# Norm factors of queries a and b moved into the exponential, their sums taken by token, rotations on VectorE, latents' squares added by GpSimd

## The chip, the cores and the metric

The kernel runs on one core of a Trainium2 chip. The metric is device time in microseconds (us) of one execution; lower is better. The engines are TensorE (PE, matrix products; PEld is its load of the stationary operand), VectorE (DVE), ScalarE (ACT), GpSimd (POOL) and SyncE (SP, which issues the transfers of the weights).

## The reference, cut to what matters

A first block (pooling, convolutions, gates, a gated feed-forward part) makes x from 256 tokens. Then two layers of a second model run over these 256 latent tokens and 256 context tokens. The change is in the second model's projections and attention:

```python
u = h @ w_in
qa, ka, va, qb, kb, vb, cq, ckv, kpe, z = jnp.split(u, split_points(), axis=-1)
qa = rms(heads(qa, 8), qn_a);  ka = rms(heads(ka, 8), kn_a)      # per head of 64
qb = rms(heads(qb, 12), qn_b); kb = rms(heads(kb, 4), kn_b)
qc = rms(heads(rms(cq, qa_norm) @ w_qb, 6), qn_c)                # cq has 768 columns
kvc = heads(rms(ckv, kva_norm) @ w_kvb, 6)                       # ckv has 512 columns
...
qb = apply_rope2d(qb, cos, sin); kb = apply_rope2d(kb, cos, sin) # latents only
# attention of each head group
s = q @ k * scale (+ bias or mask); p = softmax(s); o = p @ v
```

`rms(x, w)` is `x * rsqrt(mean(x*x) + eps) * w` over a head's 64 columns. Group a adds a position bias to the scores of latents, group b a band mask and a sink per head. Layer 1 needs no context queries, so the queries are 512 tokens wide in layer 0 and 256 in layer 1; keys are always 512 wide.

## The kernel before, in words

Activations lie transposed in SBUF: 128 columns of a head group on the partitions, tokens along the free axis. The weights stream through eight slots of 128x1024 elements (a quarter of a weight block each; SyncE loads a slot as soon as TensorE has used it). To keep precision at the fast rate each quarter is split: ScalarE writes the rounded high part (`whi`, L866), VectorE subtracts for the low part (`wlo`, L1332), and TensorE makes three products a chunk (high by high L2168, high by low of the activations L2169, low by high L2172). An output tile is 128 columns wide and takes two quarters, 48 products; this is a step. ScalarE and VectorE prepare quarters three ahead (`AHEAD`), PSUM has four banks for tiles. Every engine runs one order, written out by Python.

`projections(name, l)` (L600 on) sets that order for stage a (12 tiles: 4 of queries, 4 of keys, 4 of values), b (10 tiles: 6, 2, 2) and c (11 tiles of the latents ckv, kpe and cq, 12 of keys and values, 9 of queries), by lists of items for each step. In c of layer 0, and of layer 1, VectorE also makes products of streamed rows for the conditioning (L1845, L1859).

For every tile of queries and keys in a and b there is a job: VectorE copies the tile from PSUM (L1897), ScalarE squares it (L880) and rounds the square (L882), VectorE (layer 0 and the first group, L1866) or GpSimd (layer 1, L2837) makes the square's low part, TensorE multiplies both by a matrix of ones in two 64-row blocks (L2291, L2292), so that each row of a head holds the head's sum; VectorE takes mean (L1360), ScalarE the root (L895), VectorE the reciprocal (L1363) and the scaling with the gain (L1372). In b a rotation follows: VectorE swaps rows (L1920), GpSimd multiplies by sin and cos and adds (L2845 to L2848). TensorE waits for the eighth rotation before it attends.

The latents' norms (`lora`, jobs ckv and cq) take one full-precision product with ones for each of their 4 and 6 chunks (L2299, two records each), from squares that ScalarE writes into four buffers.

Stage c already takes its sums of keys and queries by token: the squares are the stationary operand, a column or two of ones streams (L2487), so the sums land with tokens on the partitions; a query's factor goes into the exponential as its scale (`q_factor`) and, negated, into the row maximum (`q_minus`).

The attention of a and b lies beside the gates' projections (`z_beside`): for a pair of heads and 128 queries come scores (TensorE, L2521), bias (L1951) or mask (L1958), maximum (L1960, L1966, L1968), exponential (ScalarE, L1224, with its row sum), normalisation (VectorE, L1985), transposes (TensorE, L2532, copied by ScalarE, L1233) and the product with the values (L2547). TensorE waits for a pair's exponential before the next pair's scores.

## Time and profile before

| | us |
|---|---|
| median of 3 runs (3268.28 to 3268.73) | 3268.7 |
| the profiled execution | 3265.98 |
| its span in the trace | 3264.2 |
| TensorE busy | 3220.0 (99%) |
| VectorE busy | 2299.4 (70%) |
| ScalarE busy | 1429.2 (44%) |
| GpSimd busy | 669.2 (21%) |

The table is read so: the span is from the first to the last instruction of one execution. An engine is busy while an instruction of it is under way; matrix products overlap in their pipeline, so a product's own duration is longer than the distance to the next one, and a busy TensorE is not TensorE at its peak. The second model runs from about 1620 us to the end.

### The profile page before, as it was taken

The numbers are of one execution on the slowest core, as the hardware profiler recorded it, in microseconds if no ns is written. First come the engines' busy times: TensorE is split into PE (matmuls) and PEld (weight loads), VectorE is DVE, ScalarE is ACT, GpSimd is POOL, SyncE is SP. The second block draws the span as 40 slices with busy tenths as digits, with TensorE's granted clock in tenths as the row PEclk, the third lists the DMA queues.
The fourth block names the chain that finished last, engine by engine and source line by source line (L and its number), as shares of the span: only waits on it lengthen the run. The fifth ranks groups of instructions, "written<-read, shape, count | busy, mean of one in ns | idle before, by whom it ended". The sixth has DMA issues, their size and how long they took to land.

```text
span 3264.2 us, 56041 instructions
## 1 busy us (share of the span) xinstructions
PE 3220.0 (99%) x20212; PEld 2763.4 (85%) x20212; DVE 2299.4 (70%) x3399; ACT 1429.2 (44%) x2193; POOL 669.2 (21%) x600
## 2 busy tenths in 40 slices
PE   8999999999999999999999999999999999999999
PEld 8999999998998777889888777777878888888878
DVE  7887877567786776777766766566658776776765
ACT  5444445445444343444543433532352363543453
POOL 4999930111450000000300011000001100210000
PEclk9999999999999999999999999999999999999999
DMA  6555555565577777777733222134316553324435
GB/s 220 182 181 185 184 184 187 184 211 187 194 246 258 250 254 256 248 253 244 256 105 113 102 92 83 53 135 140 105 65 213 199 175 113 133 97 142 154 102 177
DMA packets 159873, 559.71 MB, mean 171 GB/s; under 512 B 17552, under 2 KB 23840, under 8 KB 159264
## 3 DMA queue, kind: packets, MB, share of 16 engines
q1 hardware_dynamic: 154144, 534.60, 48.1%
q0 software_dynamic: 5504, 22.04, 2.0%
q8 instruction: 150, 2.46, 0.3%
q14 instruction: 75, 0.61, 0.1%
HBM read 550.26 MB, written 6.31 MB: 171 GB/s over the span
## 4 chain that ended last, share of the span: by engine, by line
PE 89%; DVE 5%; ACT 2%; issue 1%; DVEq 1%; ACTq 0%; DMA 0%; POOL 0%; POOLq 0%; SPq 0%
PE psum L2168 17%; PE psum L2172 17%; PE psum L2169 17%; PE psum L2195 15%; PE psum L2196 7%; PE psum L2379 3%; PE psum L2521 2%; PE psum L2547 2%; PE psum L2532 2%; PE psum L2224 2%; PE psum L2380 2%; DVE wlo L1332 1%; PE psum L2299 1%; DVE rst L1363 1%; DVEq L1318 1%
## 5 line engine op out<-in xcount | busy, mean ns | idle before, releaser
L1332 DVE TENSOR_TENSOR wlo<-raw,whi 128x1024 fp32r<-128x1024 f32 (+3 forms) x844 | 1037.0, 1235 | 379.7 <-ACT whi L866 348.9
L866 ACT ACTIVATE whi<-raw 128x1024 fp32r<-128x1024 f32 (+3 forms) x844 | 863.3, 1029 | 949.9 <-PE psum L2172 465.3
L2168 PE MATMUL psum<-hcat,whi 128*128 128x256 f32 (+1 forms) x3436 | 1122.7, 327 | 4.9 <-DVE wlo L1332 4.2
L2172 PE MATMUL psum<-hcat,wlo 128*128 128x256 f32 (+1 forms) x3436 | 1109.4, 323 | 0.0
L2169 PE MATMUL psum<-hcat,whi 128*128 128x256 f32 (+1 forms) x3436 | 1109.3, 323 | 0.0
L2195 PE MATMUL psum<-hcat,whi 128*128 128x512 f32 x2048 | 724.2, 397 | 0.1
L2168 PEld LDWEIGHTS psum<-hcat,whi 128*128 128x128 f32 x3436 | 653.2, 190 | 72.9 <-issue 16.1
L2172 PEld LDWEIGHTS psum<-hcat,wlo 128*128 128x128 f32 x3436 | 653.1, 190 | 51.4
L2169 PEld LDWEIGHTS psum<-hcat,whi 128*128 128x128 f32 x3436 | 653.5, 190 | 49.4 <-issue 0.7
L2196 PE MATMUL psum<-hcat,wlo 128*128 128x256 f32 x2048 | 573.3, 280 | 0.0
L2195 PEld LDWEIGHTS psum<-hcat,whi 128*128 128x128 f32 x2048 | 384.3, 188 | 105.9 <-issue 17.2
L2196 PEld LDWEIGHTS psum<-hcat,wlo 128*128 128x128 f32 x2048 | 386.6, 189 | 0.1
L2722 POOL TENSOR_SCALAR tap<-glu,par 128x255 f32<-128x255 f32 (+9 forms) x150 | 203.9, 1359 | 0.3 <-issue 0.3
L2379 PE MATMUL psum<-thirdcat,whi 128*128 128x512 f32 x512 | 182.9, 401 | 0.0
L2709 POOL TENSOR_TENSOR thirdcat<-tmp,thirdcat 128x256 fp32r<-128x256 f32 x43 | 51.3, 1194 | 613.5 <-ACT thirdcat L920 613.5
L2724 POOL TENSOR_TENSOR conv<-conv,tap 128x255 f32<-128x255 f32 (+9 forms) x150 | 149.1, 994 | 22.1 <-issue 0.3
L2380 PE MATMUL psum<-thirdcat,wlo 128*128 128x256 f32 x512 | 143.0, 279 | 0.0
L2761 POOL TENSOR_TENSOR racc<-racc,rsq 128x256 f32<-128x256 f32 (+1 forms) x64 | 82.9, 1295 | 240.2 <-ACT rsq L932 215.8
L2379 PEld LDWEIGHTS psum<-thirdcat,whi 128*128 128x128 f32 x512 | 96.1, 188 | 38.9 <-DVE X L1714 9.2
L1363 DVE RECIPROCAL rst<-rst 128x512 f32<-128x512 f32 (+1 forms) x39 | 106.8, 2738 | 25.9 <-ACT rst L895 25.9
L1897 DVE COPY qkv<-psum 128x512 f32<-128x512 f32 (+1 forms) x78 | 49.4, 633 | 81.0 <-PE psum L2172 80.9
L1224 ACT ACTIVATE probs<-psum,stat 128x512 f32<-128x512 f32 (+1 forms) x120 | 72.4, 606 | 70.7 <-DVE stat L1966 70.7
(307 smaller groups left out, 3647.3 us busy)
## 6 DMA issues: line engine op xcount, KB each, us to landing
raw<-in_stream SPq DMA_DIRECT2D x978, 512.0 KB, 3.9
raw<-in_stream SPq DMA_DIRECT2D x18, 384.0 KB, 3.0
raw<-in_stream SPq DMA_DIRECT2D x24, 256.0 KB, 2.9
resid_dram<-X POOLq DMA_DIRECT2D x2, 2048.0 KB, 9.4
crow<-c_dram POOLq DMA_DIRECT2D x4, 1024.0 KB, 9.1
bias<-in_natten POOLq DMA_DIRECT2D x16, 256.0 KB, 2.9
X<-resid_dram POOLq DMA_DIRECT2D x4, 1024.0 KB, 6.2
raw<-in_stream SPq DMA_DIRECT2D x16, 192.0 KB, 2.4
```

The source lines that it names most:

```text
L866: act.activation(whi[:, c % HI_SLOTS, 0:n], raw[:, slot, 0:n], ACT.Copy).then_inc(hi_ready, 1)
L1332: vec.tensor_tensor(wlo[:, slot, 0:n], raw[:, slot, 0:n], whi[:, c % HI_SLOTS, 0:n].bitcast(F32), ALU.subtract).then_inc(lo_ready, 1)
L1363: vec.reciprocal(r, r)
L2168: pe.matmul(dst, h, cat[:, kk, c0:c0 + width], start=(q == 0 and k == 0), stop=False)
L2169: pe.matmul(dst, h, cat[:, kk, c0 + loff:c0 + loff + width], start=False, stop=False)
L2172: last = pe.matmul(dst, l_, cat[:, kk, c0:c0 + width], start=False, stop=(q == nq - 1 and k == nch - 1))
L2195: pe.matmul(psum[:, bank, :].rearrange("p (l c) -> p l c", l=2), h, both, start=first, stop=False)
L2196: return pe.matmul(psum[:, bank, 0:S], l_, both[:, 0, :], start=False, stop=last)
L2379: pe.matmul(psum[:, bank, :], h, thirdcat[:, kk, :], start=first, stop=False)
L2380: return pe.matmul(psum[:, bank, 0:S], l_, thirdcat[:, kk, 0:S], start=False, stop=last)
L2722: pool.tensor_scalar(tap[:, t % 2, 0:S - t], pick(glu, c, 0, S - t), wt, None, ALU.mult)
L2724: pool.tensor_tensor(pick(conv, c, t, S), pick(conv, c, t, S), tap[:, t % 2, 0:S - t], ALU.add)
```

## The change

The queries of a and b are no longer scaled. ScalarE squares a query tile in full precision (in b straight from PSUM, where VectorE's copy then applies the gain), TensorE sums the squares by token (`qcol`), and once per stage VectorE and ScalarE make all factors (`q_factors`, `qstat`). They go into exponential and maximum as in c; the bias of a is multiplied by the factor's inverse instead, one head at a time; the sink needs its own operation. In a the queries' gain goes into the keys' weight. The rotations of b are made by VectorE alone. Of the latents' squares the first is the accumulator, GpSimd adds 3 (ckv) and 4 (cq) others, and TensorE makes 1 and 2 products in place of 4 and 6. Key jobs stay as they were, in both layers two steps behind their tile.

```diff
-        SPLIT = ("qn_a", "kn_a", "qn_b", "kn_b")
+        SPLIT = ("kn_a", "kn_b")
+        LORA_SUMS = {"ckv": (3,), "cq": (2, 3)}
+        LORA_ADDS = {"ckv": (0, 3), "cq": (3, 4)}
...
-                srcs = [whole(qkv[:, base + k, 0:w]) for k in range(count)]
+                srcs = [whole(sq[:, n, 0:w]) for n in LORA_SUMS[name]]
...
+                for t in range(nq_):
+                    at_(t + 1, "qsq", t)
+                    at_(t + 2, "qcol", t)
+                    if name == "b":
+                        at_(t + 1, "rope", ROPES_OF[f"b{l}"][t])
+                at_(nq_ + 2, "qstat")
...
-                at_(4, "sq", ckv, 0, 4, 3)
-                at_(5, "sum", ckv, 0, 4)
+                for m in range(4):
+                    at_(m + 1, "part", ckv, m, l, m)
+                at_(5, "sum", ckv, 0, 1)
...
-                at_(9, "sq", cq, 0, 3, 7)
-                at_(10, "sum", cq, 0, 3)
-                at_(k0, "sq", cq, 3, 6, 10)
-                at_(k0 + 1, "sum", cq, 3, 6)
+                for m in range(6):
+                    at_(6 + m, "part", cq, m, l, 5 + m)
+                at_(k0, "sum", cq, 0, 1)
+                at_(k0 + 1, "sum", cq, 1, 2)
...
+            def q_square(l, name, t, src):
+                n = q_no(name, l, t)
+                if n >= 4:
+                    act.wait_ge(qsq_used, n - 3)
+                act.activation(sq[:, n % 4, 0:chunks_w(l)], src, ACT.Square).then_inc(qsq_ready, 1)
...
+                    elif name == "b" and u < Q_TILES["b"]:
+                        vec.wait_ge(qsq_ready, q_no("b", l, u) + 1)
+                        vec.tensor_scalar(dst[:, j, 0:w], ps, pv("qn_b", l), None, ALU.mult).then_inc(psum_free, 1)
...
+            def q_factors(name, l):
+                k, nq_ = 2 * l + (name == "b"), Q_TILES[name]
+                st = q_mean(nq_, l)
+                nb = chunks_w(l) // P
+                vec.wait_ge(qsq_used, q_no(name, l, nq_))
+                sums_ = psum[:, 6, 0:8 * nq_].rearrange("p (h b) -> p h b", b=4)[:, :, 0:nb]
+                vec.tensor_scalar(st, sums_, 1.0 / HD, EPS, ALU.mult, ALU.add).then_inc(q_mean_ready, 1)
+                vec.wait_ge(q_root_ready, k + 1)
+                if name == "a":
+                    vec.tensor_scalar(q_inverse[:, :, :], st[:, :, 0:2], HD ** 0.5, None, ALU.mult)
+                    fence()
+                vec.reciprocal(st, st)
+                fence()
+                for dst, f in ((q_factor, HD ** -0.5), (q_minus, -HD ** -0.5)):
+                    vec.tensor_scalar(dst[:, 0:2 * nq_, 0:nb], st, f, None, ALU.mult)
+                fence()
...
-                        if r in ROPES_OF[f"b{l}"]:
-                            if it[2] >= 2:
-                                vec.wait_ge(rope_done, it[2] - 1)
-                            vec.stream_shuffle(t, ropes[r], SWAPPED)
-                            vec.drain().then_inc(swapped_ready, 1)
-                            continue
...
-                    vec.scalar_tensor_tensor(ps[:, :, 0:S], bias[:, n % BIASES, :, :], 1.0 / u["scale"], ps[:, :, 0:S],
-                                             ALU.mult, ALU.add)
+                    for h in range(2):
+                        vec.scalar_tensor_tensor(ps[:, h, 0:S], bias[:, n % BIASES, h, :],
+                                                 q_inverse[:, 2 * u["c"] + h, u["q0"] // P:u["q0"] // P + 1],
+                                                 ps[:, h, 0:S], ALU.mult, ALU.add)
...
-                    vec.scalar_tensor_tensor(negmax, top_, -u["scale"], sinks[:, u["sink"]:u["sink"] + 4:3], ALU.mult,
-                                             ALU.min).then_inc(max_ready, 1)
+                    vec.tensor_tensor(negmax, top_, minus, ALU.mult)
+                    fence()
+                    vec.tensor_tensor(negmax, negmax, sinks[:, u["sink"]:u["sink"] + 4:3], ALU.min).then_inc(max_ready, 1)
...
+                        for b in range(chunks_w(l) // P):
+                            last = pe.matmul(psum[:, 6, 8 * t + b:8 * t + b + 8:4], sq[:, n % 4, P * b:P * b + P],
+                                             halves[:, 0::HD], start=True, stop=True)
+                        last.then_inc(qsq_used, 1)
...
-                        if kind == "b":
-                            pe.wait_ge(rope_done, 8 * l + 8)
...
+            def lora_adds(l, name, j):
+                a0, adds = LORA_ADDS[name]
+                acc, w = jobs[j]["srcs"][0][0], jobs[j]["width"]
+                for m in range(1, adds + 1):
+                    a = 7 * l + a0 + m - 1
+                    pool.wait_ge(part_ready, 9 * l + (0 if name == "ckv" else 4) + m + 1)
+                    pool.tensor_tensor(acc, acc, sq[:, a % 2, 0:w], ALU.add)
+                    pool.drain().then_inc(part_used, 1)
+                pool.drain().then_inc(sq_ready, 1)
...
                 if l == 0:
                     pool.wait_ge(gate0_mods, ROW_CHUNKS)
                     crow0_load(1)
+                for name in ("ckv", "cq"):
+                    lora_adds(l, name, JOBS_OF[f"{name}{l}"][0])
```

## Rows read from the trace of the kernel before

**Rows 1.** The page, part 1: busy us (share of the span) and instructions.

```profile
PE 3220.0 (99%) x20212; PEld 2763.4 (85%) x20212; DVE 2299.4 (70%) x3399; ACT 1429.2 (44%) x2193; POOL 669.2 (21%) x600
```

**Rows 2.** Stretches: length, busy us per engine (PE to POOL), clock, DMA share, GB/s.

```profile
2969.00:3075.00 106.00, 105.86 (x608) 92.28 (x604) 69.90 (x94) 33.85 (x46) 0.00 (x0) 1.00 0.51 179
```

**Rows 3.** Timeline, VectorE, a0: start, duration, engine, line, shape [idle before <-releaser].

```profile
1710.98 0.69 DVE L1897 COPY qkv<-psum 128x512 f32<-128x512 f32 x1 [1.80 <-PE psum L2172]
...
1722.37 0.69 DVE L1897 COPY qkv<-psum 128x512 f32<-128x512 f32 x1 [1.80 <-PE psum L2172]
```

**Rows 4.** Timeline, TensorE: the sums of squares in b0 and b1, steps 2 to 9 and 2 to 6.

```profile
1909.46 0.39 PE L2291 MATMUL psum<-sq_hi,halves_r 128*128 128x512 f32 x1
...
1991.78 0.47 PE L2291 MATMUL psum<-sq_hi,halves_r 128*128 128x512 f32 x1 [0.28 <-DVE sq_hi L1866]
...
2817.43 0.28 PE L2291 MATMUL psum<-sq_hi,halves_r 128*128 128x256 f32 x1
...
2823.41 0.28 PE L2291 MATMUL psum<-sq_hi,halves_r 128*128 128x256 f32 x1
...
2844.05 0.36 PE L2291 MATMUL psum<-sq_hi,halves_r 128*128 128x256 f32 x1 [1.07 <-POOL sq_hi L2837]
```

**Rows 5.** Timeline, TensorE, c0: two groups of column sums, 12 products between them.

```profile
2299.98 0.95 PE L2487 MATMUL psum<-con,csq 128*128 128x1 f32 x8
...
2303.66 0.95 PE L2487 MATMUL psum<-con,csq 128*128 128x1 f32 x8
```

**Rows 6.** Timeline, TensorE: the latents' sums, ckv in c0, the first of cq in c1.

```profile
2205.91 3.59 PE L2299 MATMUL psum<-sq,con 128*128 128x512 f32 x8
...
3055.88 1.46 PE L2299 MATMUL psum<-sq,con 128*128 128x256 f32 x6
```

**Rows 7.** Timeline, VectorE, c0: the mean of cq's squares.

```profile
2282.73 0.69 DVE L1360 TENSOR_SCALAR cq_rst<-psum 128x512 f32<-128x512 f32 x1 [0.67 <-PE psum L2299]
```

**Rows 8.** Timeline: GpSimd in a1; VectorE in c1, copy of tile 9 and product.

```profile
2651.07 0.74 POOL L2837 TENSOR_TENSOR sq_hi<-sq,sq_hi 128x256 fp32r<-128x256 f32 x1 [39.42 <-ACT sq_hi L882]
...
3059.12 0.42 DVE L1897 COPY qkv<-psum 128x256 f32<-128x256 f32 x1
...
3059.67 1.30 DVE L1859 CUSTOM_DVE_ANT_0 psum<-raw,crow,gate_half 128x1024 f32<-128x1024 f32 x1
```

**Rows 9.** Timeline, b0: VectorE beside GpSimd; and from the page, part 5, all wlo.

```profile
1976.79 1.81 DVE L1332 TENSOR_TENSOR wlo<-raw,whi 128x1024 fp32r<-128x1024 f32 x1
1977.48 1.72 POOL L2846 TENSOR_TENSOR qkv<-qkv,con 128x256 f32<-128x256 f32 x1
...
L1332 DVE TENSOR_TENSOR wlo<-raw,whi 128x1024 fp32r<-128x1024 f32 (+3 forms) x844 | 1037.0, 1235 | 379.7 <-ACT whi L866 348.9
```

**Rows 10.** Timeline, VectorE: a rotation (c0) from shuffle to end; a small operation (c1).

```profile
2287.63 0.44 DVE L1923 STREAM_SHUFFLE tmp<-cqk 128x256 f32<-128x256 f32 x1
...
2289.48 0.76 DVE L1932 COPY cqk<-cqk 128x512 f32<-128x512 f32 x2
...
3135.45 0.16 DVE L1680 TENSOR_SCALAR q_minus<-col_stat 128x4 f32<-128x4 f32 x1
```

**Rows 11.** Groups by line and shape: count | busy us, mean ns | idle before.

```profile
L1224 ACT ACTIVATE probs<-psum,stat 128x512 f32<-128x512 f32 x80 | 54.0, 677 | 50.2 <-DVE stat L1966 50.2
L1224 ACT ACTIVATE probs<-psum,stat,q_factor 128x512 f32<-128x512 f32 x24 | 18.4, 775 | 5.0 <-DVE stat L1964 4.9
```

**Rows 12.** Timeline: b0, probabilities and transposes; b1, second scores, later exponential and scores.

```profile
2029.11 0.88 DVE L1985 TENSOR_SCALAR probs<-probs,stat 128x512 f32<-128x512 f32 x2
2030.25 1.09 PE L2532 MATMUL psum<-con,probs 128*128 128x128 f32 x8
...
2899.49 1.13 PE L2521 MATMUL psum<-qkv 64*128 64x512 f32 x4 [0.87 <-ACT probs L1224]
...
2921.54 0.19 ACT L1224 ACTIVATION_READ_ACCUMULATOR probs<-psum,stat 128x1 f32 x1
2922.72 1.13 PE L2521 MATMUL psum<-qkv 64*128 64x512 f32 x4
```

More of the change, by code:

```diff
@@ L294, in build @@
     region("consts", CO["invcount"] * 4)
-    region("small", (96 * 2 + KD * 3 + 24 + LAYERS * H_B + S + 120) * 4)
+    region("small", (96 * 2 + KD * 3 + 24 + LAYERS * H_B + S + 192) * 4)
     region("work", 16 * KIB)
@@ L605, in build, with q_no @@
                 vts += [(src[:, base + k, :], k * P) for k in range(count)]
+        Q_TILES = {"a": 4, "b": 6}
+        def q_no(name, l, t):
+            return 10 * l + (4 if name == "b" else 0) + t
         def projections(name, l):
@@ L679, in projections @@
                         at_(q0_ + i + 2, "qfin", i // 3)
-            order = ("sum", "kpe", "fin", "rope", "vt", "cat", "col", "kfin", "spread", "qfin", "sq", "csq", "sqlo")
+            order = ("qcol", "sum", "kpe", "qstat", "fin", "rope", "vt", "cat", "col", "kfin", "spread", "qfin", "qsq", "sq", "part", "csq", "sqlo")
             for u in items:
@@ L890, in squares, with lora_square @@
                     act.activation(sq[p0:p1, n % 4, 0:J["width"]], ap, ACT.Square).then_inc(sq_ready, 1)
+            def lora_square(j, m, l):
+                J = jobs[j]
+                a0, adds = LORA_ADDS[J["name"]]
+                src = qkv[:, LORA_BASE[J["name"]] + m, 0:J["width"]]
+                if m == 0:
+                    act.activation(J["srcs"][0][0], src, ACT.Square).then_inc(part_ready, 1)
+                elif m <= adds:
+                    a = 7 * l + a0 + m - 1
+                    if a >= 2:
+                        act.wait_ge(part_used, a - 1)
+                    act.activation(sq[:, a % 2, 0:J["width"]], src, ACT.Square).then_inc(part_ready, 1)
+                else:
+                    act.wait_ge(part_used, 7 * l + a0 + adds)
+                    act.wait_ge(sq_used, J["src0"] + 1)
+                    act.activation(J["srcs"][1][0], src, ACT.Square).then_inc(sq_ready, 1)
             def root(j):
@@ L1168, in projected @@
                 for u, (s, nq) in enumerate(t[0:2] for t in tiles_):
+                    if name == "b" and 0 < u <= Q_TILES["b"]:
+                        t = u - 1
+                        act.wait_ge(weights_used, tiles_[t][0] + tiles_[t][1] - 1 + SLOTS + 1)
+                        q_square(l, name, t, psum[:, BANK[first + t], 0:chunks_w(l)])
                     hi(SQ.index(s) + AHEAD)
@@ L1172, in projected @@
                             pair(JOBS_OF["hc1"][0], m)
+                    if name == "a" and 0 < u <= Q_TILES["a"]:
+                        act.wait_ge(psum_free, copied(first, u - 1))
+                        q_square(l, name, u - 1, qkv[:, u - 1, 0:chunks_w(l)])
                     for_heads(items[u], first, l)
@@ L1176, in projected @@
                 return items[len(tiles_):]
+            def q_square(l, name, t, src):
[3 more added lines that the diff above has]
+                act.activation(sq[:, n % 4, 0:chunks_w(l)], src, ACT.Square).then_inc(qsq_ready, 1)
             def for_heads(todo, first, l):
-                for it in sorted(todo, key=lambda it: it[0] not in ("sq", "csq")):
+                for it in sorted(todo, key=lambda it: it[0] not in ("sq", "part", "csq")):
                     if it[0] == "fin":
@@ L1205, in for_heads @@
                     elif it[0] == "sq":
+                        name = "b" if jobs[it[1]]["roped"] else "a"
                         act.wait_ge(psum_free, copied(first, it[4]))
+                        act.wait_ge(qsq_used, q_no(name, l, Q_TILES[name]))
                         squares(it[1], it[2], it[3])
+                    elif it[0] == "qstat":
+                        k = 2 * l + (first == T0[f"b{l}"])
+                        nq_ = Q_TILES["ab"[k % 2]]
+                        act.wait_ge(q_mean_ready, k + 1)
+                        st = q_mean(nq_, l)
+                        act.activation(st, st, ACT.Sqrt).then_inc(q_root_ready, 1)
+                    elif it[0] == "part":
+                        act.wait_ge(psum_free, copied(first, it[4]))
+                        lora_square(it[1], it[2], l)
             def probabilities(no):
@@ L2863, in _ @@
                 biases_in(f"a{l}")
-                for n, j in enumerate(JOBS_OF[f"b{l}"]):
-                    if l:
-                        square_low(j)
-                    if n:
-                        rope(l, n - 1)
-                rope(l, 7)
+                for j in JOBS_OF["b1"] if l else ():
+                    square_low(j)
                 if l == 0:
```

81 lines of the change are left out of this document (40 added, 41 removed).

## The prediction

> **What bounds the kernel now.** I read the page first. The engine table [rows 1] shows TensorE with work in flight for 3220.0 of 3264.2 us and VectorE for 70%: what TensorE has to issue, plus the short moments in which it waits, is the time. The table of stretches [rows 2] says the same of one changed stage (context stage of layer 1: 105.86 of 106.00 us at full granted clock). So I read the change as TensorE's work added and removed, and then look at each handover to it: does the new order of VectorE, ScalarE and GpSimd arrive later or earlier than TensorE asks? I call the stages a0, b0, c0, a1, b1, c1 (head group and layer), and a step the time of one output tile.
>
> **Sums of the queries' squares (a and b, 10 tiles per layer).** Before, each tile has two multiplications by the block matrix, as wide as the tile's own. In a0 a step of 48 + 2 such multiplications takes 11.39 us, from one copy to the next [rows 3], so 0.228 each and 0.46 for the two; at half width (layer 1) a step is 5.98 us [rows 4], 0.12 each, 0.24 for the two. After, each tile has 4 (layer 0) or 2 (layer 1) multiplications with the squares as the loaded operand and two columns streaming. The form exists in stage c: from one group of four (eight records) to the next it is 3.68 us with 12 wide multiplications between [rows 5], 12 x 0.228 = 2.73, so a group costs 0.93 to 0.95; half as many cost 0.47. Added: 10 x (0.93 - 0.46) + 10 x (0.47 - 0.24) = 4.7 + 2.3 = **+6.9 us** of TensorE. One column streams there and two here; the weight load is the same, so I keep the value. Bounds: 5 (if the last load hides) and 9 (if each group pays the restart again).
>
> **Latents' squares.** A full-precision sum over one 512-wide chunk: four took 3.59 [rows 6]; less the tail of the last one (about 0.16) that is 0.86 each. At 256 three took 1.46 [rows 6], 0.43 each. Ten sums become three per layer: 7 x 0.86 = 6.0 in c0, 3 x 0.86 + 4 x 0.43 = 4.3 in c1, together -10.3 us. Not all of it reaches the end.
> c0: 2 x 2.57 go at steps 5 and 10, 0.86 comes at step 11, so 4.3 is gained by the end of tile 11. The last sum is 1.7 shorter, but VectorE waited for it only 0.67 [rows 7]; after that its reciprocal and the key rotation set the order as before. VectorE has idle in c0 that covers the earlier start. **-4.95 us** (bounds -6.0 and -3).
> c1: here VectorE is behind. It copies tile 9 at 3059.12 [rows 8], 3.2 us after TensorE has finished it (the sums of step 10 start at 3055.88 [rows 6]). Until now nothing waited for this copy at once; now the first sum of step 11 needs the square of tile 9 and GpSimd's add of it. That add takes at least 0.74 at this width (GpSimd subtracting tiles of the same shape, [rows 8]). In b0 a wlo subtraction that meets a GpSimd product takes 1.81 us, where all 844 have a mean of 1.24, and the GpSimd product 1.72 against 0.74 for a subtraction of its size [rows 8, 9]: they hold each other up. So I let each of the three adds before that copy cost VectorE its 0.74: copy at 3061.3, or 3060.3 if 1 us of its wait for weights goes, since TensorE frees the slots earlier. To the copy come 0.42 for itself, 1.4 for the vector product (1.30 and its fence [rows 8]) that the add has to pass, 0.74 for the add: 3062.9 to 3063.9. Then the sum (0.43) and tile 11 (2.73) end at 3066.1 to 3067.1. Before, tile 11 ended at 3055.88 + 1.30 (three sums) + 5.74 + 2.73 (tiles 10 and 11) = 3065.65. Loss 0.4 to 1.4; without any hold-up it would be a gain of about 2. I take **+0.5 us**, because rows 9 show the hold-up; bounds -3.4 (all of TensorE's saving) and +4.
> The Trainium skill, "SBUF — State Buffer", section "Who interferes with whom", has a rule that speaks against the move: a VectorE instruction with two SBUF inputs and a GpSimd instruction that reads SBUF exclude each other for a whole instruction, whichever began first. By that rule no overlap is left and c1 comes out at its upper end, 1.4; by free overlap it would be -2. The trace agrees with the rule [rows 9].
>
> **VectorE's steps in a and b.** Removed per query tile: mean, wide root round trip, reciprocal, scaling, low half. What that frees matters only where VectorE was late. In b0 TensorE needed 82.32 us for seven steps [rows 4], against 7 x 11.39 = 79.73: 2.6 late. In b1 26.62 us for four steps [rows 4] against 23.92: 2.7 late, and those are query steps. In a0 it was not late: the copy waited 1.80 for TensorE [rows 3].
> After, query steps are light, a rotation on VectorE included (1.85 us from its shuffle to the copy behind it [rows 10]). The first key step isn't: behind the new wait for ScalarE's root of the factors stand the key's mean, root, wide reciprocal, scaling, its rotation, the second wlo and the next key's low half, for which TensorE waits in layer 0. The factors are six operations on 128x48 or less, one 0.16 [rows 10], with one trip to ScalarE: I estimate 1.6 us, between 0.8 (five times 0.16) and 2.7 (0.8 more than a rotation). a0: 11.39 - 1.80 + 1.6 = 11.2: it just fits, **+0.1**. b0: 11.2 + 1.85 + fences = 13.4 against 11.39: TensorE waits 2.0 once, **-2.6 + 2.0 = -0.6** (bounds -2.0 and +1.5). The next step needs no low half; the attention beside the gates starts half a tile later, and VectorE is ready by then. b1: GpSimd makes the low half, nothing waits, **-2.7** (bounds -2.9 and -1).
>
> **What else moves.** ScalarE squares b's queries from PSUM ahead of its whi copy, and VectorE's copy waits for that: some 0.6 us later for whi, wlo and the copy, with two steps of weights and four banks in hand, nothing for TensorE; if that cover were gone, 0.6 a step. GpSimd waits for seven squares a layer; behind it in c0 stands only the load of the context's c row, which the output stage needs, so it is hidden; without that cover it would be the few us of one add. No other transfer moves: the biases and the first rows keep their places.
>
> **Attention of a and b.** An exponential with its scale from a column took 775 ns, with a constant 677 [rows 11]: +0.1 per head, 0.2 per pair. Pairs of b get one more small operation and a fence between maximum and exponential, 0.25; pairs of a with a bias get it in two halves, 0.1. So the chain scores to exponential grows by 0.45 in b and 0.2 to 0.3 in a. Cover: in b1's steady state the scores start 0.99 after the exponential before them has ended [rows 12]: hidden. But the second pair of b1 already waited 0.87 [rows 12], and its successor has little spare: +0.7 in b1, +0.45 in a1 and +0.35 in a0 likewise. In b0 the transposes start 0.26 after the probabilities are scaled [rows 12]; eight pairs are like that, 8 x (0.45 - 0.26) = 1.5. Together **+3.0 us**, bounds +1 and +6.
>
> **Sum.** 6.9 - 4.95 + 0.5 + 0.1 - 0.6 - 2.7 + 3.0 = +2.25 us. The rows are of one execution of 3265.98 us (span 3264.2), 2.7 below the median of the runs shown, 3268.7. The difference is added to the median: **3271.0 us**. What a measurement of this kernel can tell from no change is about 0.2%, 6.5 us: this is within it.
>
> **Rivals.**
> 1. TensorE's own work alone counts and every wait hides. 6.9 - 10.3 - 2.6 - 2.7 = -8.7: 3260.0. For it: 99% busy. Against: VectorE is late in c1 and in b0's first key step, shown above. Chance 0.08.
> 2. GpSimd's lock bites twice. Each add before the copy of tile 9 holds up a second vector instruction (3 x 0.74 = 2.2), and of the three adds of c1 that are twice as wide (an estimate of 1.5 each from [rows 8]) half is not absorbed before step 5, 2.2 more: 3271.0 + 4.4 = 3275.4. Place: copy of tile 9 in c1. It decides once that copy is over 2 us later than now. For it: rows 9, both sides lengthened. Against: in the early steps VectorE waits for weights and can absorb it. Chance 0.14, slower than before, about half of it by over 0.2%.
> 3. The attention chain becomes the bound (the other side, clearly slower). If it grows by more than the 0.99 us of spare in b1, and all of the 0.26 in b0, all 36 pairs of b show their 0.45: 16.2 instead of the 2.2 counted, 3285. It decides when the chain grows by about 1 us per pair, twice my value. For it: rows 12. Against: the parts have rows and add to 0.45. Chance 0.07.
> 4. That the change does not do what it says (the column sums are no cheaper than what they replace) is in my sum already.
>
> **Chances and range.** The forecast's case has 0.71, its own range 3266 to 3275. Faster by over 0.2%: rival 1, 0.07. Slower by over 0.2%: rival 3, 0.07, half of rival 2, 0.07, and 0.03 from the forecast's upper end: 0.17. The rest, 0.76, is within 0.2%. The range of 8 in 10 leaves out rival 3 and most of rival 1 and takes in rival 2: 3264 to 3277.
>
> **What the profile after should show.** Groups of 8 and 4 records of the column sums with 0.93 and 0.47 us to the next tile; b1's query steps at 5.98 + 0.23 without waits; one wait of about 2 us for the low half in b0, at the second key; in c1 a wait of TensorE for GpSimd before the first sum of step 11; wlo at its mean of 1.24 throughout b0 but longer beside the adds; exponentials at 775 ns in all pairs. Wrong would be: no wait at the GpSimd sum in c1 (rival 1), or waits for the exponentials in every pair of b (rival 3).

## The result

| | before | after |
|---|---|---|
| median (lowest to highest) | 3268.24 (3264.88 to 3268.73, 6 runs) | 3284.51 (3281.63 to 3286.06, 6 runs) |
| ratio | | 1.0051, 95% interval 1.0041 to 1.0061 |
| profiled execution, span | 3265.98, 3264.2 | 3285.89, 3283.8 |

Slower by 16.3 us. The forecast was 3271.0 with a range of 3264 to 3277. The third rival names about this time, 3285, but by a way that the traces don't show (0.45 us in each of 36 pairs of b). The two profiled executions lie 19.9 apart, since the one before is 2.3 below its median and the one after 1.4 above; beside the experiments the changed kernel came out the same again (3284.62) and the kernel before somewhat faster (3265.7 to 3266.9).

The page's first part shows nothing alarming (to be held against [rows 1]): VectorE has 52 us less, GpSimd 42 less, TensorE 8 more.

```profile
PE 3228.4 (98%) x20264; PEld 2773.0 (84%) x20264; DVE 2247.5 (68%) x3448; ACT 1418.6 (43%) x2157; POOL 627.5 (19%) x556
```

The stretch of [rows 2] is no longer full either: waits of TensorE, two of them beside GpSimd's adds.

```profile
2969.00:3075.00 106.00, 103.78 (x665) 91.21 (x662) 69.36 (x95) 38.28 (x55) 9.86 (x6) 1.00 0.52 180
```

**TensorE's waits** from 1640 to 3200 us, after (engine, line, who released it: us in total, times, the longest):

```profile
PE psum L2573 <- ACT csq L1244: 4.9, 3, 2.6
...
PE psum L2369 <- DVE sq_hi L1926: 4.1, 2, 3.0
...
PE psum L2560 <- ACT sq L1226: 3.8, 1, 3.8
...
PE psum L2250 <- DVE gate_half L1919: 1.0, 1, 1.0
PE psum L2250 <- DVE ada_t L1919: 0.9, 1, 0.9
...
PE psum L2377 <- POOLq L2933: 0.8, 1, 0.8
```

and the lines of before that answer to the first two:

```profile
PE psum L2487 <- ACT csq L1194: 3.0, 2, 1.7
...
PE psum L2291 <- POOL sq_hi L2837: 2.1, 2, 1.1
...
PE psum L2291 <- DVE sq_hi L1866: 1.8, 4, 1.0
```

Three single waits stand out: 3.8 us in a1 for the square of the first query tile, 3.0 in b0 for the low half of the second key, 2.6 in c0 for a column group. **Behind each the granted clock of TensorE is at half**, the 1.2 GHz level: in this trace it falls 0.4 to 0.9 us before the late multiplication starts, and stays down for 6.8 us. Stretches of the trace after (the seventh field is the granted clock): the first is behind the wait in b0, the third behind that in c0, the fourth behind that in a1, the last in c1 behind waits of 0.76 and 0.99. The second, right after the first fall, is at full clock again.

```profile
1997.00:2003.00 6.00, 5.58 (x13) 4.50 (x14) 5.30 (x5) 0.63 (x1) 0.00 (x0) 0.50 0.04 16
2004.00:2010.00 6.00, 6.00 (x28) 4.96 (x27) 3.37 (x7) 1.06 (x1) 0.00 (x0) 1.00 0.27 89
2297.00:2303.00 6.00, 5.68 (x17) 4.85 (x18) 2.87 (x8) 2.26 (x5) 0.00 (x0) 0.50 0.00 0
2659.00:2665.00 6.00, 5.57 (x26) 5.57 (x27) 4.24 (x6) 4.31 (x8) 0.00 (x0) 0.50 0.01 4
3092.00:3095.00 3.00, 3.00 (x9) 2.38 (x9) 1.26 (x6) 0.74 (x3) 0.00 (x0) 0.53 0.05 20
```

The reader is to see the counts: 13 multiplications in six microseconds at half clock, 28 in six at full clock, with TensorE "busy" in both. The busy share can't show this loss. Summed over stretches of 5 us as (1 - granted clock) x 5, the trace after loses 3.4 + 3.4 + 3.4 + 1.7 = 11.9 us of full clock between 1640 and 3250 us; the trace before loses none there.

**Where the time is, by stretch.** I cut each trace at rows of TensorE's timeline: the multiplication that ends the first stage's wait of 1.39 (1643.35 before, 1642.15 after), the first scores of each attention, the first product of a1, the last multiplication. Every stretch holds the same work in every kernel but for its edits.

| stretch, us | before | after | e1 | e5 | e6 | e7 | e9 | e10 |
|---|---|---|---|---|---|---|---|---|
| a0, to its scores | 144.94 | 147.88 | 147.89 | 147.85 | 147.89 | 144.98 | 144.62 | 144.62 |
| to b0's scores | 224.15 | 230.84 | 228.01 | 228.06 | 227.72 | 224.17 | 224.27 | 224.94 |
| to c0's scores | 360.37 | 360.49 | 357.49 | 358.96 | 355.22 | 353.05 | 360.40 | 362.45 |
| to a1's first product | 234.69 | 235.03 | 234.83 | 234.69 | 234.88 | 234.88 | 234.89 | 237.03 |
| to a1's scores | 147.92 | 154.37 | 151.66 | 153.18 | 148.67 | 147.93 | 147.84 | 147.83 |
| to b1's scores | 139.01 | 138.68 | 138.70 | 138.68 | 138.67 | 139.07 | 138.91 | 140.13 |
| to c1's scores | 239.66 | 242.62 | 241.05 | 241.08 | 240.81 | 239.92 | 239.58 | 241.53 |
| to the end | 126.46 | 128.10 | 128.09 | 128.10 | 128.08 | 126.46 | 128.10 | 128.09 |
| sum | 1617.20 | 1638.01 | 1627.72 | 1630.60 | 1621.94 | 1610.46 | 1618.61 | 1626.62 |

After against before: +20.8 in all, of which +6.7 to b0's scores, +6.5 to a1's, +3.0 to c1's, +2.9 in a0 and, where nothing at all was edited, +1.6 at the end. (The program ahead of the first mark is 1.2 shorter, so the spans differ by 19.6.)

### The profile page after: what moved, and what is told of

Same layout as the page of the kernel before. It is cut to its first block, busy times and chain, and to the rows that moved or that the text cites. A ratio compares the mean times of both kernels' runs of the same rounds, so it can differ in the third digit from the quotient of the medians.

```text
span 3283.8 us, 56132 instructions
## 1 busy us (share of the span) xinstructions
PE 3228.4 (98%) x20264; PEld 2773.0 (84%) x20264; DVE 2247.5 (68%) x3448; ACT 1418.6 (43%) x2157; POOL 627.5 (19%) x556
## 4 chain that ended last, share of the span: by engine, by line
PE 83%; issue 7%; DVE 5%; ACT 2%; DVEq 1%; ACTq 0%; DMA 0%; POOLq 0%; POOL 0%; SPq 0%
PE psum L2246 16%; PE psum L2250 15%; PE psum L2247 15%; PE psum L2273 15%; PE psum L2274 7%; PE psum L2457 4%; PE psum L2607 2%; PE psum L2458 2%; PE psum L2302 2%; PE psum L2633 1%; PE psum L2618 1%; DVE wlo L1391 1%; ACT probs L1283 1%; DVEq L1377 1%; DVE stat L2039 1%
## 5 line engine op out<-in xcount | busy, mean ns | idle before, releaser
L1283 ACT ACTIVATE probs<-psum,stat,q_factor 128x512 f32<-128x512 f32 (+1 forms) x156 | 108.4, 698 | 74.8 <-DVE stat L2043 74.7
L2633 PEld LDWEIGHTS psum<-probsT,vtok 128*64 128x64 f32 (+1 forms) x1040 | 70.6, 149 | 38.9 <-ACT probsT L1292 20.8
L1400 DVE SCALAR_TENSOR_TENSOR half<-up,par,half 128x255 f32<-128x255 f32 (+1 forms) x172 | 92.0, 535 | 13.3 <-issue 0.4
```

The costliest lines, as they stand in the source:

```text
L1283: last = act.activation(probs[:, no % 2, h, 0:nk], psum[:, s_bank(no) + h, 0:nk], ACT.Exp, bias=negmax, scale=scale, accum_out=stat[:, 8 + ...
```

## The experiments

My theory A: the time went into a few waits of TensorE and, as much again, into the half clock behind them. Rivals: added work, GpSimd's hold-ups, the attention chain. e1 to e4 ran beside 9 runs of the kernel before (median 3265.72), e5 to e8 beside 26 (3265.77), e9 to e11 beside 24 (3266.94).

**e1: TensorE kept busy in the three waits.**

```diff
+            def filler(dst, count):
+                for _ in range(count):
+                    pe.matmul(dst, cv("ident"), cv("cos"), start=True, stop=True)
...
+                        if name == "a" and l and t == 0:
+                            filler(psum[:, 6, 64:64 + S], 8)
                         pe.wait_ge(qsq_ready, n + 1)
```

and in the same way 6 ahead of the second key's sum of b0, 5 ahead of c0's column group.

> The changed kernel, with TensorE kept busy in its three longest waits: ahead of the waiting multiplication stand multiplications of the identity by a constant tile of 256 columns (0.43 us each, as a full-precision sum of that width), whose result is overwritten or never read: 8 before the first column sum of a1 (wait 3.75 us), 6 before the second key's sum in b0 (3.02), 5 before the third column group of c0 (2.64). No other engine's work changes, so each wait lasts as long as before. Theory A (granted clock): the trace shows TensorE's granted clock at 0.5 for 6.8 us at the end of each of these three waits, which costs about 3.3 us each; with TensorE busy the three falls are gone and the time is 10 us shorter, 3274.5 against 3284.5. Theory B (the falls of the clock come with something else, or cost nothing because TensorE is then not the bound; the 16 us are added work, GpSimd's hold-ups and the attention chain): 3284 to 3286, since fillers shorter than the wait change nothing.

3276.71 us (3275.49 to 3280.01), ratio 1.0036 [1.0023, 1.0050]; the changed kernel in e5 has 1.0053. The same three places in the trace of e1, and c1:

```profile
1990.00:2004.00 14.00, 13.67 (x61) 11.12 (x60) 12.82 (x14) 2.26 (x4) 0.00 (x0) 1.00 0.23 75
2287.00:2303.00 16.00, 15.52 (x92) 13.36 (x90) 14.03 (x24) 5.16 (x10) 0.00 (x0) 1.00 0.16 50
2648.00:2664.00 16.00, 15.70 (x119) 14.94 (x119) 11.92 (x16) 10.98 (x18) 0.00 (x0) 1.00 0.38 129
3080.00:3095.00 15.00, 14.01 (x83) 11.95 (x81) 12.52 (x27) 6.55 (x13) 0.00 (x0) 1.00 0.18 61
```

No fall is left before the last multiplication. The other engines do what they did, the waits end when they did, and yet the three stretches are 2.8, 3.0 and 2.7 us shorter than after. Behind these waits without fillers, over all traces, 12 of 13 have a fall; with fillers, none of three. In c1, where no filler stands, it is 1.6 shorter, and that fall is missing by chance (it is there in three of the six traces with those waits). 10.3 in all. By medians it is 7.9 (3284.62 of e5 less 3276.71), since an execution of the changed kernel doesn't always have all four falls, as e5 shows. The record of every execution says the same: a mean granted clock of 0.996 to 0.999 in the eleven of the changed kernel, 0.999 to 1.000 in the five of e1. Theory B, no gain from useless work, is out.

**e2: the column sums of a1 one step later.**

```diff
-                    at_(t + 2, "qcol", t)
+                    at_(min(t + (3 if l and name == "a" else 2), nq_ + 1), "qcol", t)
```

> The changed kernel with one index moved: in a1 the column sums of a query tile come one step later (tile t at step t + 3, the last at step 5), as the sums of a1's heads did before the change. Theory A (wait and clock): ScalarE's square of query 0 stands behind the context pairs and is late for step 2, not for step 3, so the 3.75 us wait and the 6.8 us at half clock behind it (3.3 us) go: -7, 3277.5. Theory B (the squares are late in every step, since ScalarE is behind in a1's first steps whatever the order): the wait moves one step on, -0 to -2, 3283 to 3284.5. If only the wait counts and the clock doesn't, -3.8: 3280.7.

3277.72 us (3276.05 to 3278.88), 1.0035 [1.0021, 1.0048]: 6.9 below e5, as theory A said. To a1's scores it takes 148.68 us in place of 154.37; what TensorE waits for there is the wait that the kernel before had too (0.75):

```profile
2658.48 0.39 PE L2246 MATMUL psum<-hcat,whi 128*128 128x256 f32 x1 [0.76 <-DVE wlo L1391]
```

**e3: the factors of b0 one step later.**

```diff
-                at_(nq_ + 2, "qstat")
+                at_(nq_ + (3 if name == "b" and l == 0 else 2), "qstat")
```

> The changed kernel with the queries' factors of b0 made one step later (step 9 in place of 8), so that they no longer stand on VectorE between the first key's copy and the low half of the second key's squares. Theory A: the wait of 3.02 us before the second key's sum shrinks by the factors' 2.5 us to about 0.5, and with it the granted clock's fall behind it goes (3.3 us): -5.8, 3278.7. Nothing waits for the factors at step 9: attention of b starts beside the next stage. Theory B (it is the first key's normalisation and rotation that are too long, not the factors): wait stays above 2 us, the clock still falls, -0.5 to -1, 3283.5 to 3284. The wait alone without clock: -2.5, 3282.

3280.77 us (3279.20 to 3281.88), 1.0043 [1.0030, 1.0057]: 3.9 below e5. In the profiled execution the stretch to b0's scores is 226.18 against 230.84: -1.9 of wait and -2.8 of clock. Less than the 5.8 expected: in c0 and a1 the falls stay, and the wait was to shrink by 2.5 and shrank by 1.9:

```profile
1995.64 0.47 PE L2369 MATMUL psum<-sq_hi,halves_r 128*128 128x512 f32 x1 [1.13 <-DVE sq_hi L1926]
```

The missing 0.6 is ScalarE's table load (item 3 below), which didn't go with the factors: in e3 it stands before the key's own root, at 1985.55, and VectorE waits 1.34 for that root where it waited 0.70 after.

**e4: the latents' sums by TensorE again**, the lines of the diff on "part", `LORA_SUMS` and `lora_adds` taken back.

> The changed kernel with the sums of the latents' squares made by TensorE again as before the change (GpSimd adds nothing); the queries' factors and the rotations stay changed. Theory A: c0 gets 6.0 us of work back, the wait before its column group falls from 2.64 to 1.72 and the granted clock doesn't fall behind it (3.3 + 0.9 less); c1 gets 4.3 back and loses waits of 0.91, 0.97, 0.76 and 1.00 and a short fall of the clock (1.7). Sum 10.3 - 4.2 - 5.3 = +0.8: 3285. Theory B (GpSimd's adds hold VectorE up so much that they are the main loss): clearly faster than the changed kernel, by 5 or more, 3279 or less. Theory C (TensorE's saved work is the gain that it was meant to be, all 10.3 of it, and the loss lies elsewhere): 3294.

3285.39 us (3284.77 to 3287.68), 1.0060 [1.0047, 1.0074], against 1.0053 of the changed kernel: no difference that can be told, and +0.8 was expected. To c0's scores it is 362.58 (after 360.49), to c1's 240.81 (after 242.62): GpSimd's adds gain 2.1 in c0 and lose 1.8 in c1, the half clock counted in both. That they were the main loss is out, and so is theory C (3294), by which TensorE's saved work would all arrive.

**e5: the changed kernel once more.**

> The changed kernel as it is, once more, as the yardstick for the runs beside it on the same chip. Both theories: 1.005 of the kernel before, TensorE's granted clock at 0.5 behind the waits in b0, c0 and a1. Theory A (the falls follow the waits) expects them at the same three places as in the first trace, though each can last 3.4 or 6.8 us, as the runs so far showed both behind the same wait of 3.02 us (e2 and e4: 1.7 us of full clock lost in b0, the first trace: 3.4). Theory B (they come by chance in time) expects them at other places.

3284.62 us (3278.90 to 3284.81), 1.0053 [1.0039, 1.0067]. Its profiled execution is the shortest of the five, and with the trace after it makes a comparison that no edit could: the same program, the same waits (3.01 in b0, 2.64 in c0, 3.76 in a1), and other falls of the clock.

```profile
1997.00:2003.00 6.00, 5.11 (x23) 4.25 (x24) 5.30 (x6) 0.63 (x1) 0.00 (x0) 1.00 0.13 53
2295.00:2301.00 6.00, 6.00 (x27) 5.04 (x27) 3.08 (x8) 2.42 (x5) 0.00 (x0) 0.72 0.01 3
2655.00:2658.00 3.00, 2.76 (x13) 2.76 (x14) 1.89 (x4) 2.08 (x3) 0.00 (x0) 0.58 0.01 3
3085.00:3095.00 10.00, 9.40 (x58) 8.35 (x59) 8.13 (x17) 4.63 (x9) 0.00 (x0) 1.00 0.19 55
```

None in b0, half as much in c0 and a1 (1.7 us of full clock each), none in c1: 3.4 lost in place of 11.9, and the stretches sum to 1630.60 in place of 1638.01. So a wait of 3 us can bring a fall and need not. Theory A's "same three places" held for two of them, and none came elsewhere.

**e6: the changed kernel mended.** The edits of e2 and e3, GpSimd's adds in layer 0 alone, and in c0 the shared key's weighting and rotation a step earlier:

```diff
-                at_(k0 + 1, "kpe")
-                at_(k0 + 1, "rope", ROPES_OF[f"kpe{l}"][0])
+                at_(k0 + (l > 0), "kpe")
+                at_(k0 + (l > 0), "rope", ROPES_OF[f"kpe{l}"][0])
```

> The changed kernel with its idle stretches mended and its gain kept: column sums of a1 one step later (wait 3.75 gone), factors of b0 one step later (3.02 to 1.13), in c0 the shared key's weighting and rotation one step earlier (3.3 us of VectorE's work in a step in which it waits 2.2 for TensorE, in place of 3.3 behind the reciprocal; the wait of 2.64 before the column group to about 0.5), and GpSimd's adds in layer 0 alone. Theory A: waits 3.0 + 1.9 + 2.1 and the clock's 9.3 behind them, 1.8 of c1 (wait and clock against TensorE's own sums): 18 less than the changed kernel, so 1 to 2 us below the kernel before. Theory B (the column sums' +6.9 and the attention chain's +3 are what made it slow, and don't go): work +6.9 - 6.0 + 3.0 against waits of b gone 5.3, and half of the loss stays: 7 or more above the kernel before.

3268.80 us (3268.16 to 3271.96), 1.0010 [1.0001, 1.0019]: 15.8 below e5 and 3 above the kernel before, where 1 to 2 below it was expected. By the table the places mended are mended (to c0's scores 355.22, to a1's 148.67); c0's stretch gains 5.2 over before, and what is lost is 2.95 in a0, 3.6 to b0's scores, 0.75 to a1's, 1.15 to c1's and 1.6 at the end. Of the 3.6 one part is a fall of the clock, 1.7 us of full clock lost at 1886.9 behind a wait of 1.8. e9 and e10 go after the end and the attention.

**e7: only what gained, on the kernel before:** GpSimd's adds in layer 0 and the two lines moved above.

> The kernel before with two edits alone: in layer 0 GpSimd adds the latents' squares (three sums of 0.86 us in place of ten), and in c0 the shared key's weighting and rotation stand one step earlier on VectorE, ahead of the wide reciprocal. Theory A: 6.0 us of TensorE's work go, and the wait of 1.72 before the column group with it, so no long wait and no fall of the clock: -7.7, 0.9976 of the kernel before, 3258 beside 3265.7. Rival (GpSimd's adds delay VectorE in c0 as in c1, where TensorE got three waits of 0.8 to 1.0 from it): -3 to -5. Rival (the earlier rotation delays the copy of tile 11 by its whole 3.3 us and the wait comes back before the latents' own sums): -4.

3258.25 us (3257.01 to 3260.44), 0.9974 [0.9964, 0.9983]: 7.5 faster than the kernel before, 7.7 expected, and faster than both kernels. The column group of c0 waits 0.33 in place of 1.72:

```profile
2283.63 1.05 PE L2528 MATMUL psum<-con,csq 128*128 128x1 f32 x8 [0.33 <-ACT csq L1232]
```

To c0's scores it is 7.3 shorter than before; every other stretch is within 0.3 of it.

**e8: GpSimd's adds in both layers, on the kernel before.**

> The kernel before with GpSimd's adds of the latents' squares in both layers and nothing else: the part of the change that saves TensorE's work, by itself. By the stages of the first traces: c0 6.0 less work, 0.9 more wait before the column group (1.72 to 2.64), and behind that wait either a fall of the clock (3.1) or none; c1 4.3 less work, waits of 0.91, 0.97, 0.76 and 1.00 new, and 1.5 of clock or none. Theory A: -0.3 with both falls, -5 with none; I take -2. Theory C (TensorE's work is the time): -10.3.

3263.79 us (3262.44 to 3265.61), 0.9992 [0.9983, 1.0001]: -2.0, with no change just inside the interval. That it is the very value taken is partly luck: -2 was a middle between both falls and none, and the trace has two falls of 1.7 us of full clock, in c0 and in c1. Of 10.3 us of TensorE's work two arrive: to c0's scores it is 356.91, 3.5 less than before, where 6.0 of work went; to c1's it is 241.50, 1.8 more, though 4.3 of work went. The timeline of TensorE in c1 shows what eats them there:

```profile
3043.89 0.36 PE L2203 MATMUL psum<-hcat,wlo 128*128 128x256 f32 x1 [0.91 <-DVE ada_t L1890]
3050.86 0.35 PE L2203 MATMUL psum<-hcat,wlo 128*128 128x256 f32 x1 [0.99 <-DVE gate_half L1890]
3057.56 0.67 PE L2330 MATMUL psum<-sq,con 128*128 128x256 f32 x2 [0.32 <-POOLq L2891]
...
3070.24 1.05 PE L2518 MATMUL psum<-con,csq 128*128 128x1 f32 x8 [0.97 <-ACT csq L1222]
```

The first two are waits for vector products of a gate's rows. These keep their 1.29 us here; what grows beside GpSimd's add is the `wlo` behind each of them, from 1.22 in the kernel before to 1.74:

```profile
3042.78 1.47 POOL L2889 TENSOR_TENSOR sq<-sq 128x256 f32<-128x256 f32 x1 [5.51 <-ACT sq L914]
...
3043.60 1.74 DVE L1363 TENSOR_TENSOR wlo<-raw,whi 128x1024 fp32r<-128x1024 f32 x1
```

So VectorE's round comes to 7.0 us (its copies start at 3034.84, 3041.84 and 3048.82; 0.9 of it is a wait for ScalarE's `whi`), and TensorE, whose step is 5.74, waits for it. In c0 of the trace after it is a product that grows; the same product just before took 1.29 us:

```profile
2273.47 1.82 POOL L2931 TENSOR_TENSOR sq<-sq 128x512 f32<-128x512 f32 x1 [8.03 <-ACT sq L922]
...
2274.33 2.06 DVE L1905 CUSTOM_DVE_ANT_0 psum<-raw,crow,gate_half 128x1024 f32<-128x1024 f32 x1
```

**e9: the layout line alone, on the kernel before.**

```diff
-    region("small", (96 * 2 + KD * 3 + 24 + LAYERS * H_B + S + 120) * 4)
+    region("small", (96 * 2 + KD * 3 + 24 + LAYERS * H_B + S + 192) * 4)
```

> The kernel before with one line of the change alone: the region of small tensors in SBUF is 72 floats longer, so what lies behind it starts 288 bytes further on; nothing else. In the last 80 us (output stage of layer 1) every kernel with the new factors so far shows 0.3533 us per pair of multiplications (512 and 256 wide) where the kernel before and e7 and e8, without them, show 0.3467, at the same granted clock: 1.6 us over the stage. Theory A (the place of the data makes it): 0.3533 here too and +1.6 us. Theory B (something else of the new factors does, the number or place of TensorE's instructions for instance): 0.3467 and no difference, within 0.5 us of the kernel before.

3267.20 us (3266.41 to 3270.28), 1.0002 [0.9993, 1.0011]: the times can't tell it from before. The trace can. Sixty microseconds of the output stage, first the kernel before:

```profile
3180.00:3240.00 60.00, 60.00 (x348) 52.91 (x347) 39.15 (x48) 24.07 (x23) 0.00 (x0) 1.00 0.63 212
```

then e9:

```profile
3180.00:3240.00 60.00, 60.00 (x341) 51.99 (x341) 38.03 (x46) 22.91 (x22) 0.00 (x0) 1.00 0.62 207
```

341 multiplications in place of 348 at the same granted clock, and 128.10 us to the end in place of 126.46. All nine traces with that line have 128.07 to 128.10, the four others 126.45 or 126.46, so the 1.6 us belong to it; every other stretch is within 0.3 of before. Theory A holds for the place; why the place matters to TensorE there stays open.

**e10: the attention part alone, on e9:** scale and factors from columns that hold the constants.

```diff
-                    scale = u["scale"]
+                    scale = ab_factor[:, 0:1]
...
-                    vec.scalar_tensor_tensor(negmax, top_, -u["scale"], sinks[:, u["sink"]:u["sink"] + 4:3], ALU.mult,
-                                             ALU.min).then_inc(max_ready, 1)
+                    vec.tensor_tensor(negmax, top_, ab_minus[:, 0:2], ALU.mult)
+                    fence()
+                    vec.tensor_tensor(negmax, negmax, sinks[:, u["sink"]:u["sink"] + 4:3], ALU.min).then_inc(max_ready, 1)
```

> The kernel of e9 with the attention part of the change alone: scale of the exponentials of a and b from a column (filled once with the constant), the bias of a added in two halves with a column as factor, and in b the maximum scaled and compared with the sink in two operations with a fence. Norms, sums and rotations are those of the kernel before. Theory A (my term, mis-sized at most by one): +3.0 over e9, of which 0.35 in a1 (wait before the second pair 0.76 to 1.11), 0.4 in b1 (0.87 to 1.27), 0.8 in a0, the rest in b0 beside c0's tiles. Theory B (the first traces' difference in c0 and at the ends of stages is of other origin): under +1. Theory C (every pair of b pays 0.45): +16.

3276.42 us (3271.94 to 3277.72), 9.2 over e9 by medians; ratio to before 1.0022 [1.0012, 1.0032], where e9 has 1.0002. The stretches are 8.0 longer than e9's: 0.7 to b0's scores, 2.05 to c0's, 2.1 to a1's first product, 1.2 to b1's, 1.95 to c1's. The 2.1 stand where e10 edits nothing: a wait for `ada_t` of 1.79 (0.86 in e9, 0.63 to 1.11 in the other traces) and a fall of the clock behind it, 1.7 us of full clock lost. Whether the attention part causes them isn't shown. The four stretches in which a's and b's attention lies give 5.9, twice my term and far from theory C's 16. In b1 two waits show it (0.87 before at the first, none at the second):

```profile
2907.41 1.13 PE L2529 MATMUL psum<-qkv 64*128 64x512 f32 x4 [1.28 <-ACT probs L1227]
...
2913.32 1.13 PE L2529 MATMUL psum<-qkv 64*128 64x512 f32 x4 [0.56 <-ACT probs L1227]
```

**e11: e7 with the rotations of b1 by VectorE.**

> e7 (GpSimd's adds in layer 0, the shared key's rotation one step earlier in c0) with the rotations of b1 by VectorE in place of GpSimd, norms by tile as before. Theory A: in b1 TensorE waited 1.04 and 1.07 us for the low half of the squares, which stands on GpSimd behind its rotation; without rotations it is there in time, VectorE carries 1.3 more per step of 5.98 and has the idle for it: -2.1 against e7, 3256.2 beside 3265.8 (ratio 0.9970). Theory B (VectorE is itself late in b1: reciprocal 1.75, two wlo of 1.4, copy, scaling, rotation come to 8 us per tile in 5.98 us steps or near it): the wait moves to VectorE, 0 to +4 against e7.

3260.15 us (3258.68 to 3263.12), 0.9978 [0.9969, 0.9988]: not faster than e7; the stretch to b1's scores is 139.66 against 139.07. The waits in b1 are still there, and longer than 1.04 and 1.07:

```profile
2830.30 0.35 PE L2332 MATMUL psum<-sq_hi,halves_r 128*128 128x256 f32 x1 [1.32 <-POOL sq_hi L2878]
...
2838.16 0.36 PE L2332 MATMUL psum<-sq_hi,halves_r 128*128 128x256 f32 x1 [1.58 <-POOL sq_hi L2878]
```

GpSimd's rows say why, first e7, then e11:

```profile
2828.00 0.72 POOL L2878 TENSOR_TENSOR sq_hi<-sq,sq_hi 128x256 fp32r<-128x256 f32 x1 [0.18 <-issue]
```

```profile
2829.43 0.72 POOL L2878 TENSOR_TENSOR sq_hi<-sq,sq_hi 128x256 fp32r<-128x256 f32 x1 [7.06 <-ACT sq_hi L903]
```

In e7 the low half did stand behind the rotation, which ended at 2827.82, a microsecond after ScalarE had the high half ready (2826.82). In e11 GpSimd is idle and starts at once, but ScalarE waits for VectorE's copy, and VectorE's round has grown from 7.3 us a tile (copies at 2818.16 and 2825.47) to 7.8 (2820.20 and 2828.00), against 5.98 of TensorE. So theory B holds: take GpSimd's delay away and VectorE's own round binds. The name behind the arrow is only the last link.

## Why the prediction was wrong

The sum of the prediction by stretch, beside what e1 shows, which is the changed kernel with the clock at full (e1 less before): a0 +2.0, measured 2.95; to b0's scores +2.6, 3.86; to c0's -3.45, -2.88; to a1's first product 0, 0.14; to a1's scores +0.9, 3.74; to b1's -0.9, -0.31; to c1's +1.2, 1.39; end 0, 1.63. So the terms gave 2.3 where 10.5 was measured, and half clock, +10.3 in the traces and 7.9 by medians, had no term at all. (The column sums' 4.7 + 2.3 add up to 7.0, not the 6.9 written; that changes nothing.) In the order of their size:

1. **The step that failed most: a wait was priced at its length.** The prediction foresaw an idle TensorE in b0 and wrote "TensorE waits 2.0 once" and nothing more. The trace before has no fall in the second model, and [rows 2] a clock of 1.00, so I took it as given; yet it loses 1.7 us of full clock near 845 us, which showed that the clock of this kernel can fall. Runs e1 and e5 show that the same waits with and without the fall differ by 2.7 to 3.0 us each. The Trainium skill describes such falls in "TensorE: Matmul & The Clock Gate", section "HAM oscillation — how this bites in real kernels": idle stretches between bursts take the array back to the half-rate state. The traces agree, and add that a wait of 1.0 in c1 had a fall behind it in three traces, and one of 3.0 in b0 had none in one.
2. **a1 was not worked out.** "VectorE's steps in a and b" treats a0, b0 and b1. In a1 the change brought the sums from three steps behind their tile to two (queries and keys; the section on the change says two steps "in both layers" and overlooks that the kernel before had three here), and ScalarE's square stands behind the context pairs. ScalarE's and TensorE's rows of the trace after:

```profile
2657.30 1.07 ACT L979 ACTIVATE hfull<-scaled,ada_t,gain 128x256 f32<-128x256 f32 x2
...
2658.45 0.63 ACT L982 ACTIVATE hcat<-hfull 128x512 fp32r<-128x512 f32 x1
2658.98 0.40 ACT L1226 ACTIVATE sq<-qkv 128x256 f32<-128x256 f32 x1
...
2659.43 1.02 PE L2560 MATMUL psum<-con,sq 128*128 128x2 f32 x4 [3.75 <-ACT sq L1226]
```

The tile had been copied by 2654.95 (2654.53 + 0.42); its square came four microseconds later. 3.0 us of wait more than before, and e2 takes it away with one index.
3. **b0: the mechanism was right, the size was off.** +1.2 of waits (3.02 against four that sum to 1.8) where -0.6 stood. The factors were estimated at 1.6 us; from the first small operation to the key's own mean it is 2.53:

```profile
1985.38 0.20 DVE L1975 TENSOR_SCALAR col_stat<-psum 128x48 f32<-128x48 f32 x1
1985.44 1.28 ACT L1265 ACT_TABLE_LOAD   x1
1986.74 0.24 ACT L1265 ACTIVATE col_stat<-col_stat 128x48 f32<-128x48 f32 x1
1987.02 0.46 DVE L1980 RECIPROCAL col_stat<-col_stat 128x48 f32<-128x48 f32 x1 [1.44 <-ACT col_stat L1265]
...
1987.91 0.69 DVE L1419 TENSOR_SCALAR rst<-psum 128x512 f32<-128x512 f32 x1
```

Half of it is ScalarE's table load for the square root, 1.28, which comes when a root follows the exponentials of a's attention, and which the estimate, built from a small operation of 0.16, left out. The kernel before has the same load in b0 (L895, at 1912.02), but at its first query tile (behind it TensorE waits 0.95 at 1921.95); the change moved it to the tightest step of the stage, where TensorE waits 3.02. The Trainium skill has it in "ScalarE: Activation LUTs", section "What ACT_TABLE_LOAD costs", at about 1283 ns; the trace agrees. The drain of about 1380 ns that the page adds to it isn't in this trace, where the root begins 1.30 us after the load has begun. Of e3's 1.13 of wait that stays, 0.6 is this load again; the rest is the key's own norm and rotation, which no run here takes apart. The same low half in a0, where "it just fits, +0.1" stood, cost 1.09.
4. **Attention +3.0: half of what it is by itself** (e10: 5.9), since I counted only the pairs whose spare time I had a row for. Within the changed kernel it is less: to c0's scores e6 is 2.2 over e7, to c1's 1.15 over before.
5. **The end, +1.6:** a line of the diff that I read as harmless (e9).
6. **What held.** The column groups; from the start of one to the next in b0, after:

```profile
1911.93 0.95 PE L2560 MATMUL psum<-con,sq 128*128 128x2 f32 x8
1923.76 0.95 PE L2560 MATMUL psum<-con,sq 128*128 128x2 f32 x8
```

11.83 us, less 48 multiplications of 0.228 is 0.89, against 0.93. b1's query steps are 6.20, against 5.98 + 0.23. The work saved in c0: -5.1 (e1's 357.49 against e4's 362.58, both without a fall), -4.95 predicted. The adds in c1: +0.24 (241.05 against 240.81), +0.5 predicted, with the wait for GpSimd where it was said (0.76), though those for the row products were not. Exponentials with a column as scale, in all pairs (775 said):

```profile
L1283 ACT ACTIVATE probs<-psum,stat,q_factor 128x512 f32<-128x512 f32 x104 | 79.7, 769 | 54.7 <-DVE stat L2043 54.7
```

GpSimd's adds, for which I had only guessed at their size (1.5):

```profile
L2931 POOL TENSOR_TENSOR sq<-sq 128x512 f32<-128x512 f32 x10 | 17.8, 1778 | 226.8 <-ACT sq L922 226.8
```

wlo in b0 after, where the rotations on GpSimd are gone (1905 to 2003 us):

```profile
L1391 DVE TENSOR_TENSOR wlo<-raw,whi 128x1024 fp32r<-128x1024 f32 x16 | 19.6, 1225 | 22.8 <-ACT whi L885 22.1
```

and beside the adds of c1 (3030 to 3095 us), longer, as was said:

```profile
L1391 DVE TENSOR_TENSOR wlo<-raw,whi 128x1024 fp32r<-128x1024 f32 x11 | 15.0, 1366 | 6.2 <-ACT whi L885 6.1
```

Of the rivals, the first (-8.7) fell at the waits. The second's sign, the copy of tile 9 in c1 more than 2 us later, didn't come: counted from b1's first scores it stands at 166.1 after (3075.57) and 164.7 before (3059.12), 1.4 later and so within the forecast; c1's further loss in that trace is the clock. The third has a true core, the chain of attention, at 5.9 of its 16 us.

## What to carry to other kernels

An idle stretch of a TensorE that is otherwise always busy can cost its length again in half clock (here 2.7 to 3.0 us behind waits of 2.6 to 3.8): price each new wait with both, and give a range for it, since the same program has the fall in one execution and not in another. Before moving a step, list every stage in which its index changes, and who stands ahead of it on its own engine; one index (e2, e3) was worth 4 to 7 us. Work taken from the bounding engine gains only where its next handover isn't already a wait: the same adds were worth 5 us in c0 and nothing in c1, and moving the shared key's rotation out of the chain behind the reciprocal made c0's whole (e7, 7.5 us).

## What the runs showed of the hardware that I had not expected

- The granted clock falls at waits from 1.0 to 3.8 us, between 0.9 us before the wait's end and 2.1 after it (after b0, e5 c0), and not each time: behind the wait of 1.80 in a0's attention it fell in e2 and e6 (1.7 us of full clock lost) and not in the six other traces with that wait; behind that of 3.0 in b0 it lost 3.4, 1.7, 1.7 and 0 in four traces (after, e2, e4, e5).
- Multiplications whose result nobody reads shortened the kernel by 7.9 us (medians of e1 and e5).
- 288 bytes more ahead of some SBUF tensors slow TensorE's output stage of layer 1 by 2% (348 to 341 multiplications in 60 us) and no other stretch; the cause is open.
- A vector product of three operands went from 1.29 to 2.06 us beside a GpSimd add, which itself took 1.82.
